# The turned inverse of a recurrent core: transposes on VectorE in place of products on TensorE

## The reference, cut to what matters

```python
def step(state, inp):
    r_t, w_t, k_t, v_t, kk_t, b_t = inp
    sa = jnp.einsum('bhij,bhj->bhi', state, -kk_t)
    state = (state * w_t[:, :, None, :] + sa[..., None] * b_t[:, :, None, :]
             + v_t[..., None] * k_t[:, :, None, :])
    return state, jnp.einsum('bhij,bhj->bhi', state, r_t)
_, y = lax.scan(step, state0, tuple(tm(z) for z in (r, decay, k, v, kk, b)))
```

## Time and profile before

| | |
|---|---|
| median of 3 runs | 1928.11 us |
| the profiled execution, its own time | 1930.77 us |
| its span in the profile | 1929.1 us |
| mean granted TensorE clock | 0.992 of full speed |
| busy: TensorE, weight loads, VectorE, ScalarE, GpSimd | 1866.0, 1615.2, 1263.4, 998.6, 111.6 us |

### The profile page before, as it was taken

The page is one execution under the profiler, slowest core; times in us unless marked ns, Lnnn a source line. Parts: engine busy times, 40 slices in busy tenths (PEclk is TensorE's granted clock), DMA queues, the critical chain, the costliest instruction groups (busy, mean ns, idle before and its releaser), DMA issues. The chain is left out here.

```text
span 1929.1 us, 33999 instructions
## 1 busy us (share of the span) xinstructions
PE 1866.0 (97%) x14028; PEld 1615.2 (84%) x14028; DVE 1263.4 (65%) x1830; ACT 998.6 (52%) x1554; POOL 111.6 (6%) x133
## 2 busy tenths in 40 slices
PE   7999998999999999999979999999999989999999
PEld 5888887999888888889879998888899987776787
DVE  5575776675666566657757756655888755335796
ACT  5444683554544454447645554444766535334674
POOL 1000006000000000000050000000020000000000
PEclk9999999999999999999999999998999989999999
DMA  9765440343666566654305446653534136767893
GB/s 378 286 235 188 143 151 25 139 170 131 251 230 228 182 232 248 222 175 155 109 4 207 170 177 219 244 199 114 178 130 155 64 153 262 290 281 288 316 374 152
DMA packets 53189, 378.75 MB, mean 196 GB/s; under 512 B 5992, under 2 KB 6176, under 8 KB 7856
## 3 DMA queue, kind: packets, MB, share of 16 engines
q1 hardware_dynamic: 44592, 320.30, 45.2%
q0 software_dynamic: 8448, 56.32, 7.3%
HBM read 375.53 MB, written 1.06 MB: 195 GB/s over the span
## 5 line engine op out<-in xcount | busy, mean ns | idle before, releaser
L355 DVE TENSOR_TENSOR weights_split<-ring,weights_split 128x1024 fp32r<-128x1024 f32 x456 | 540.0, 1227 | 165.2 <-ACT weights_split L345 165.0
L345 ACT CAST weights_split<-ring 128x1024 fp32r<-128x1024 f32 x456 | 454.3, 1048 | 180.5 <-PE ps L378 164.9
L376 PE MATMUL ps<-weights_split,act 128*128 128x512 f32 (+1 forms) x896 | 334.6, 373 | 12.7 <-DVE weights_split L355 12.6
L378 PE MATMUL ps<-weights_split,act 128*128 128x512 f32 (+1 forms) x896 | 329.6, 368 | 0.0
L377 PE MATMUL ps<-weights_split,act 128*128 128x512 f32 (+1 forms) x896 | 329.2, 367 | 0.0
L376 PEld LDWEIGHTS ps<-weights_split,act 128*128 128x128 f32 x896 | 169.1, 189 | 41.0 <-DVE weights_split L355 12.6
L2280 DVE TENSOR_TENSOR expert_split<-ring,expert_split 128x1024 fp32r<-128x1024 f32 x144 | 169.7, 1222 | 51.5 <-ACT expert_split L2204 48.7
L378 PEld LDWEIGHTS ps<-weights_split,act 128*128 128x128 f32 x896 | 169.0, 189 | 28.6
L377 PEld LDWEIGHTS ps<-weights_split,act 128*128 128x128 f32 x896 | 169.3, 189 | 26.3
L376 PE MATMUL ps<-act,weights_split 128*128 128x256 f32 x608 | 173.9, 286 | 0.3
L377 PE MATMUL ps<-act,weights_split 128*128 128x256 f32 x608 | 169.8, 279 | 0.0
(11 more groups left out here) (549 smaller groups left out, 3484.6 us busy)
## 6 DMA issues: line engine op xcount, KB each, us to landing
ring<-stream SPq DMA_DIRECT2D x300, 1024.0 KB, 4.8
stretch<-ada_in POOLq DMA_DIRECT2D x24, 1024.0 KB, 5.6
small_weights<-stream POOLq DMA_DIRECT2D x12, 1024.0 KB, 9.2
tokens_room<-stream POOLq DMA_DIRECT2D x12, 1024.0 KB, 9.0
y<-c_in POOLq DMA_DIRECT2D x4, 512.0 KB, 5.9
act_room<-mem_in SPq DMA_DIRECT2D x2, 1024.0 KB, 5.3
consts<-w_consts SPq DMA_DIRECT2D x1, 1280.0 KB, 11.5
x<-x_in SPq DMA_DIRECT2D x1, 1024.0 KB, 4.9
```

The lines of the kernel that those rows point to most:

```text
L345: core.nc.scalar.copy(self.hi[:, self.place(i), part], core.slot(chunk)[:, part]).then_inc(self.rounded.sem, 1)
L355: core.nc.vector.tensor_tensor(self.lo[:, self.place(i), part], core.slot(chunk)[:, part], self.hi[:, self.place(i), part].bitcast(F32), A ...
L376: nc.tensor.matmul(out, lhs[0], rhs[0], start=start, stop=False, **kw)
L378: return nc.tensor.matmul(out, lhs[1], rhs[0], start=False, stop=stop, **kw)
```

## The change

The turned inverse of levels 1 to 4 is no longer a product. ScalarE copies X of both tiles out of PSUM; then VectorE reads the same banks and writes the turned blocks with its transpose of 32x32 blocks, in three instructions per tile: one for the heads at even places on all 128 partitions, and one for each half of the partitions for the others, whose halves are exchanged. Each covers 256 elements per partition. Because X consists of blocks of 32x32 up to level 4, the transposes within such blocks turn all of it. `level_ax` of the next level waits for these transposes. At level 5 the turned inverse is still a product (`last_turned`). The places of heads in X, G and the turned inverse now follow the level. ScalarE's side work comes behind its copies of X in each level. On VectorE, the transposes stand behind `factor` and ahead of `mask_keys`.

```diff
+        def in_bank(e, lv):
+            return 2 * (e >> 2) + crosses(e, lv)
+
+        def level_place(e, lv):
+            return 4 * crosses(e, lv - 1) + in_bank(e, lv)
+
+        def inverse(rows, t, e, lv):
+            return X[rows, t, level_place(e, lv) if lv else e, :]
+
+        def turned_level(rows, t, e, lv):
+            return turned_blocks[rows, t, crosses(e, lv - 1), in_bank(e, lv), :] if lv else xt(rows, t, e)
...
+            def turn_inverse(lv, t):
+                dve.wait_ge(x_in.sem, x_in.at((lv - 1) * TT + t + 1))
+                nc.vector.transpose(turned_blocks[:, t, :, 0:4:2, :], level_banks(t)[:, :, 0:4:2, :])
+                for cp in range(2):
+                    ins = nc.vector.transpose(turned_blocks[half(1 - cp), t, :, 1:4:2, :], level_banks(t)[half(cp), :, 1:4:2, :])
+                ins.then_inc(xt_in.sem, 1)
...
                 if lv < levels - 1:
-                    dve.wait_ge(pdone.sem, pdone.at((lv - 1) * TT + 2))
-                    nc.vector.tensor_copy(in_banks(X[:, 1]), level_banks(1)).then_inc(x_v.sem, 1)
+                    for t in range(TT):
+                        turn_inverse(lv, t)
                 if lv <= TT:
                     mask_keys(lv - 1)
...
             for lv in range(1, levels):
+                if lv < levels - 1:
+                    for t in range(TT):
+                        act.wait_ge(pdone.sem, pdone.at((lv - 1) * TT + t + 1))
+                        nc.scalar.copy(in_banks(X[:, t]), level_banks(t)).then_inc(x_in.sem, 1)
                 if lv in (3, 4):
...
-                if lv < levels - 1:
-                    act.wait_ge(pdone.sem, pdone.at((lv - 1) * TT + 1))
-                    nc.scalar.copy(in_banks(X[:, 0]), level_banks(0)).then_inc(x_s.sem, 1)
-                act.wait_ge(tdone.sem, tdone.at(lv))
-                if lv < levels - 1:
-                    ins = nc.scalar.copy(turned_inverse, ps[:, UPDATE:UPDATE + 2, :].rearrange("p w n -> p (w n)"))
...
             def level_ax(lv, t):
                 pe.wait_ge(masked.sem, masked.at(lv * TT + t + 1))
                 if lv == 1:
-                    pe.wait_ge(x_v.sem, x_v.at(t + 1))
-                elif t == 0:
-                    pe.wait_ge(x_s.sem, x_s.at(lv - 1))
+                    pe.wait_ge(x_first.sem, x_first.at(t + 1))
                 else:
-                    pe.wait_ge(x_v.sem, x_v.at(TT + lv - 1))
+                    pe.wait_ge(xt_in.sem, xt_in.at((lv - 2) * TT + t + 1))
...
                     for t in range(TT):
                         level_products(lv, t)
-                for t in range(TT):
-                    level_turned(lv, t)
+            for t in range(TT):
+                last_turned(t)
```

More of the change, by code:

```diff
@@ L1281, in rwkv_stage @@
     pdone = core.sig("level_products_ready", 2 * (levels - 2))
-    tdone = core.sig("level_products_turned_ready", levels - 1)
-    x_v = core.sig("inverse_by_vector", TT + levels - 2)
-    x_s = core.sig("inverse_by_scalar", levels - 2)
+    tdone = core.sig("last_level_turned_ready", 1)
+    x_first = core.sig("inverse_first", TT)
+    x_in = core.sig("inverse_in_sbuf", 2 * (levels - 2))
     xt_first = core.sig("inverse_turned_first", TT)
-    xt_s = core.sig("inverse_turned_by_scalar", levels - 1)
-    xt_v = core.sig("inverse_turned_by_vector", 1)
+    xt_in = core.sig("inverse_turned_in_sbuf", 2 * (levels - 2))
+    xt_s = core.sig("last_inverse_turned_by_scalar", 1)
+    xt_v = core.sig("last_inverse_turned_by_vector", 1)
     turned = core.sig("chunk_transposed", 8)
@@ L1332, in rwkv_stage @@
         turned_inverse = own[:, 1024:2048]
-        XT = turned_inverse.rearrange("p (w t s n) -> p w t s n", w=2, t=TT, s=4)
+        XT = turned_inverse.rearrange("p (t w s n) -> p t w s n", t=TT, w=2, s=4)
+        turned_blocks = turned_inverse.rearrange("p (t f q n) -> p t f q n", t=TT, f=2, q=4)
         AL = (to(2), to(3))
@@ L1357, in crosses @@
             return (e & 1) ^ (e >> 1 & lv & 1)
[L1359 to L1363, removed]
+        def in_bank(e, lv):
[6 more added lines that the diff above has]
+            return turned_blocks[rows, t, crosses(e, lv - 1), in_bank(e, lv), :] if lv else xt(rows, t, e)
         def xt(rows, t, e):
-            return XT[rows, e >> 1 & 1, t, 2 * (e >> 2) + (e & 1), :]
+            return XT[rows, t, e >> 1 & 1, 2 * (e >> 2) + (e & 1), :]
         def end_place(e):
@@ L1398, in _ @@
             tt, stt = nc.vector.tensor_tensor, nc.vector.scalar_tensor_tensor
-            turned_first = XT.rearrange("p w t (d a) n -> p w t d a n", a=2)
+            turned_first = XT.rearrange("p t w (d a) n -> p t w d a n", a=2)
             def mask_removal(t):
@@ L1417, in first_inverse @@
                 for w in range(2):
-                    tt(turned_first[:, w, t, :, 1, :], over_heads(ident64)[:, 0:2],
+                    tt(turned_first[:, t, w, :, 1, :], over_heads(ident64)[:, 0:2],
                        bank4(level_bank(t) + 1).rearrange("p (d w) n -> p w d n", w=2)[:, w], ALU.subtract)
-                tt(X[:, t], over_heads(ident64), bank8(level_bank(t)), ALU.subtract).then_inc(x_v.sem, 1)
+                tt(X[:, t], over_heads(ident64), bank8(level_bank(t)), ALU.subtract).then_inc(x_first.sem, 1)
             def first_turned(t):
                 for w in range(2):
-                    ins = tt(turned_first[:, w, t, :, 0, :], over_heads(ident64)[:, 0:2],
+                    ins = tt(turned_first[:, t, w, :, 0, :], over_heads(ident64)[:, 0:2],
                              AL[0][:, t].rearrange("p (d w a) n -> p w a d n", w=2, a=2)[:, w, 0], ALU.subtract)
@@ L1444, in _ @@
                 if lv < levels - 1:
-                    dve.wait_ge(pdone.sem, pdone.at((lv - 1) * TT + 2))
-                    nc.vector.tensor_copy(in_banks(X[:, 1]), level_banks(1)).then_inc(x_v.sem, 1)
+                    for t in range(TT):
+                        turn_inverse(lv, t)
                 if lv <= TT:
                     mask_keys(lv - 1)
-            dve.wait_ge(tdone.sem, tdone.at(levels - 1))
-            nc.vector.tensor_copy(XT[:, 1].rearrange("p t s n -> p (t s n)"), ps[:, UPDATE + 1, :]).then_inc(xt_v.sem, 1)
+            dve.wait_ge(tdone.sem, tdone.at(1))
+            nc.vector.tensor_copy(XT[:, :, 1].rearrange("p t s n -> p t (s n)"),
+                                  ps[:, UPDATE + 1, :].rearrange("p (t n) -> p t n", t=TT)).then_inc(xt_v.sem, 1)
             for t in range(TT):
@@ L1553, in _ @@
                                        ps[:, TURN + f, :].rearrange("p (t s n) -> p t s n", t=TT, s=4)).then_inc(bv_moved.sem, 1)
-                if lv < levels - 1:
-                    act.wait_ge(pdone.sem, pdone.at((lv - 1) * TT + 1))
-                    nc.scalar.copy(in_banks(X[:, 0]), level_banks(0)).then_inc(x_s.sem, 1)
-                act.wait_ge(tdone.sem, tdone.at(lv))
-                if lv < levels - 1:
-                    ins = nc.scalar.copy(turned_inverse, ps[:, UPDATE:UPDATE + 2, :].rearrange("p w n -> p (w n)"))
-                else:
-                    ins = nc.scalar.copy(XT[:, 0].rearrange("p t s n -> p (t s n)"), ps[:, UPDATE, :])
-                ins.then_inc(xt_s.sem, 1)
+            act.wait_ge(tdone.sem, tdone.at(1))
+            nc.scalar.copy(XT[:, :, 0].rearrange("p t s n -> p t (s n)"),
+                           ps[:, UPDATE, :].rearrange("p (t n) -> p t n", t=TT)).then_inc(xt_s.sem, 1)
             for t in range(TT):
@@ L1621, in level_ax @@
                 if lv == 1:
-                    pe.wait_ge(x_v.sem, x_v.at(t + 1))
-                elif t == 0:
-                    pe.wait_ge(x_s.sem, x_s.at(lv - 1))
+                    pe.wait_ge(x_first.sem, x_first.at(t + 1))
                 else:
-                    pe.wait_ge(x_v.sem, x_v.at(TT + lv - 1))
+                    pe.wait_ge(xt_in.sem, xt_in.at((lv - 2) * TT + t + 1))
                 for e, cp in quarters():
                     f = crosses(e, lv - 1)
-                    ins = mm(level_banks(t)[half(cp ^ f), f, e // 2, :], AL[lv % 2][half(cp), t, e, :],
-                             X[half(cp), t, inverse_place(e, lv - 1), :], start=True, stop=True)
+                    ins = mm(level_banks(t)[half(cp ^ f), f, in_bank(e, lv), :], AL[lv % 2][half(cp), t, e, :],
+                             inverse(half(cp), t, e, lv - 1), start=True, stop=True)
                 ins.then_inc(gdone.sem, 1)
@@ L1636, in level_products, with last_turned @@
                     pe.wait_ge(xt_first.sem, xt_first.at(t + 1))
-                else:
-                    pe.wait_ge(xt_s.sem, xt_s.at(lv - 1))
                 for e, cp in quarters():
                     f = crosses(e, lv - 1)
-                    ins = mm(level_banks(t)[half(cp), f, e // 2, :], xt(half(cp ^ f), t, e),
-                             G[half(cp ^ f), t, factor_place(e, lv - 1), :], start=True, stop=True)
+                    ins = mm(level_banks(t)[half(cp), f, in_bank(e, lv), :], turned_level(half(cp ^ f), t, e, lv - 1),
```

(11 more changed lines are left out.)

## The result

The changed kernel takes 1935.57 us, the median of 8 runs (1932.92 to 1938.24), against 1929.01 us for the kernel before in 8 runs: ratio 1.0034, 95% interval 1.0025 to 1.0043. It is slower by 6.6 us. The forecast was 1923.1, the range 1919.0 to 1933.3. So the sign was wrong, and the time lies 2.3 us above the range.

What follows compares the result with a forecast made beforehand. The prediction took delivery of TensorE's instructions to bound the level stretch. Gains of 2.9 us in layer 0 and 2.1 in layer 1, together 5.0, from 1928.1 gave 1923.1 us, range 1919 to 1933.3.

Steps and rivals of the forecast that it cites:

- the delivery of 127 products per 3.5 us: Level stretch (level 1's level_ax to last_turned): TensorE's instructions arrive in blocks, some 3.5 us per 127 products, bounding it.
- the stops: Level stretch: TensorE halts on issue inside started units, 0.45 to 1.34 us each, one block per 3.35 to 3.64 us.
- The third rival: Stops at block boundaries cost a fixed 0.8 us that no slack hides: +2.4 us per layer, 1933; chance 0.05.
- A unit of 32 products ends 0.69 after it starts, the next can start after 0.45: TensorE's unit times in us, used to sum the chain of the new level stretch.
- the four cases: Transposes priced as reads, 0.50; dearer transposes, 0.17 and 0.13; fixed stops, 0.05; slower or returning delivery stops, 0.15.
- The price of three transposes: VectorE, per level and token tile: three transposes cost 1.15 us, 1.07 from three to three, priced as PSUM reads.
- TensorE's side work in levels 3 and 4: Reads' transposes and product: halves 0.53 and 0.56 us around a 0.45 product in level 3; 0.45 and 0.44 in level 4.
- the forecast's chain: Dependent work through levels 1 to 5 of the new level stretch, ending 26.55 us after it begins.
- The second rival: Transposes cost more than reads, deciding from 1.53 us for three; up to 1933.3; chance 0.17 slower, 0.13 for 1926 to 1930.
- The masks behind the transposes: VectorE's key-product masks stand in the chain in levels 2 and 3, counted at 1.28 less 0.08 overlap and 1.20 us.
- a loss in the core goes to the end: Behind the core only TensorE is full, so time won or lost there reaches the program's end undiminished.
- the signs named: Signs of being right: transposes 0.42 to 0.48 us, 128 records for 640, at most three stops, stretches 26.6 and 27.9 us.

## Why the prediction was wrong, step by step

- What bounds the level stretch of the kernel before, the delivery of 127 products per 3.5 us: right. Two blocks more cost 7.6 and 7.75 us where 7.0 was reckoned, and in the changed kernel the stops are gone where a block lasts longer (5 packets of the instruction queue in 30 us instead of the 8 of the earlier trace rows). The third rival, stops of fixed length, is out.
- **The step that failed** is the sentence "A unit of 32 products ends 0.69 after it starts, the next can start after 0.45". It was taken from rows at a clock of 1.00 and used in a stretch in which TensorE was to wait for VectorE at every level. The prediction worked out these waits itself, and did not ask what they do to the clock. With units at 1.13 us the low clock made the changed kernel's stretches 4.9 and 2.9 us longer than they are with the waits filled, 7.8 of the 9.7 us by which they grew. None of the four cases held this mechanism.
- The price of three transposes, 1.15 us, was low: 1.38; and from three to three 1.41 where 1.07 was reckoned. The element count was the right measure for one (0.45 against 0.42); that they would overlap as the reads do was wrong. With four of the one and three of the other that is 1.9 us per layer.
- TensorE's side work in levels 3 and 4 was too short as well, at any clock. Each half of the reads' transposes was reckoned at 0.53 and 0.56 us. In the kernel before each is ten records and takes 1.11 us up to the next unit, and the unit ahead of it holds TensorE for 0.62 us, not 0.45:

```profile
323.09 0.69 PE L1629 MATMUL ps<-weights_split_room 64*64 64x64 f32 x32
323.71 0.33 PE L1598 MATMUL ps<-consts,stretch 128*128 128x128 f32 x1
323.97 0.66 PE L1595 MATMUL ps<-consts,stretch 128*64 128x128 f32 x8
324.56 0.33 PE L1598 MATMUL ps<-consts,stretch 128*128 128x128 f32 x1
324.82 0.69 PE L1629 MATMUL ps<-weights_split_room 64*64 64x64 f32 x32
```

That is 1.3 us in level 3, and in level 4, with 0.63 and 0.58 for 0.45 and 0.44, 0.3 us: 1.6 us per layer.
- So the forecast's chain at full clock should have been 26.55 + 1.9 + 1.6 = 30.1 us, and the run with the waits filled has 29.99 in layer 0 (in layer 1 it has 31.37, with stops of 2.4 us in it). With the 4.9 us of the low clock that makes 35.0, where 34.87 was measured. The kernel before has 29.47 and 29.99: even with the clock held the change had nothing to gain. That the filled run's 1927.58 us lies close to the forecast is no support for it. The second rival had the dearer transposes. Its point of decision, 1.53 us for three, was worked out from the chain of 26.55, which was 1.6 us short without them. By the same sum with 1.6 us more it falls to 1.38 us, and that is what three cost.
- The masks behind the transposes were counted, 1.2 us in each of two levels. Moving them ahead of the transposes gave 5.3 and 4.1 us of stretch, more than the 2.4 counted, since much of the low clock went with the wait for them (1.94 us idle at 325.16, then 0.50; with the masks ahead 0.97 from 320 to 330).
- That a loss in the core goes to the end: from the start of the first stretch to the end of the program 7.9 of the 9.7 us arrive. That the tail does not change: right within 0.8 us.
- Of the signs named, the transposes at 0.42 to 0.48 us, the records and the missing stops came true; stretches of 26.6 and 27.9 us did not. The granted clock was not among the signs, though it stands in every window that was read.

## What to carry to other kernels

Taking products away from TensorE and putting another engine's work into its waits can cost more than the products did, because the products that stay run at 1.2 GHz: work out from the rows how much TensorE will wait in the new stretch and which of its two clocks it will then run at, not only how long its chain is. And take every unit of that chain, side work too, from its own row: one short by half costs as much as a wrong price for the new instruction. A move to VectorE pays where the new work lies beside the chain, here by reading the copy in SBUF instead of holding the PSUM banks that the next product needs. And where TensorE issues many tiny products, count instructions: 256 records more per layer cost 7.6 us, though they are 3.6 us of TensorE's time.

## What the runs showed of the hardware

- TensorE was granted half its clock (1.2 GHz) after 4 us in which it was busy 1.94 us between waits for VectorE. Eleven unread products of 128x256 per layer in these waits kept the clock at 1.00 and made the changed kernel 8 us faster; thirty kept it at 1.00 too and made it no faster.
- A transpose of 256 fp32 elements per partition on VectorE takes 0.450 us out of PSUM (0.448 on 64 partitions) and 0.438 out of SBUF, and two in a row do not overlap (0.91 and 0.89 us).
- Where TensorE's instructions are small, a stop comes every 127 products with their weight loads, 3.35 to 3.9 us from stop to stop: 13 to 15 ns per instruction. A 64x64 fp32 record and its weight load need 14 ns for the two at full clock (32 in 0.45 us).
